# Rotary pair swap of q and k: a VectorE lane shuffle in place of a TensorE permutation matmul, with q and k of layers 3 and 4 laid out so that the two members of a pair lie 16 lanes apart

## What is computed

```python
def apply_rope(x, cos, sin):                       # layers 1 and 2
    n_freq = HEAD_DIM // 4                         # 16
    xf = x.astype(jnp.float32).reshape(*x.shape[:-1], 2, 2, n_freq)
    x1, x2 = xf[..., 0, :], xf[..., 1, :]          # pairs lie 16 apart
    cb, sb = cos[None, :, None], sin[None, :, None]
    out = jnp.stack([x1 * cb - x2 * sb, x2 * cb + x1 * sb], axis=-2)
...
def apply_rope_2(t, cos, sin):                     # layers 3 and 4
    half = QK_DIM // 2                             # 32
    t1, t2 = t[..., :half], t[..., half:]          # pairs lie 32 apart
    return jnp.concatenate([t1 * cos - t2 * sin, t2 * cos + t1 * sin], axis=-1)
```

## Time and profile before

| | |
|---|---|
| three runs | 2384.16, 2387.83, 2380.02 us; median 2384.16 |
| profiled execution | span 2381.0 us (the page gives no other time for it) |
| TensorE busy | 2312.4 us, 97% of the span |
| VectorE busy | 1349.6 us, 57% |
| ScalarE busy | 1077.6 us, 45% |
| DMA | 335.97 MB, 141 GB/s in the mean |
| mean granted TensorE clock | 0.992 |

### The profile page before, as it was taken

How to read it: one execution, slowest core, us unless ns; L and a number is a source line. 1 busy time by engine, 2 the same in 40 slices (tenths; PEclk the granted TensorE clock), 3 DMA queues, 4 the chain that set the end, 5 groups by cost and what they waited for, 6 DMA issues and landing times.

```text
span 2381.0 us, 36140 instructions
## 1 busy us (share of the span) xinstructions
PE 2312.4 (97%) x14230; PEld 1894.7 (80%) x14230; DVE 1349.6 (57%) x2393; ACT 1077.6 (45%) x2066; POOL 33.5 (1%) x40
## 2 busy tenths in 40 slices
PE   8999999999889999999999999999999999999999
PEld 6658878778857999777667788888888887798888
DVE  5454432333646767577886434534434778756776
ACT  4343422223545555545556423522323765655543
POOL 0300000000100000000000000000000000000000
PEclk9999999999999999999999999999999999999999
DMA  8473333333365555255554322222222222154554
GB/s 312 169 272 110 98 115 124 115 126 105 107 230 178 195 177 179 92 197 191 196 207 151 106 97 84 85 98 98 97 95 92 89 89 72 58 164 151 188 184 151
DMA packets 95319, 335.97 MB, mean 141 GB/s; under 512 B 10672, under 2 KB 12720, under 8 KB 95024
## 3 DMA queue, kind: packets, MB, share of 16 engines
q1 hardware_dynamic: 95152, 333.67, 41.3%
HBM read 332.58 MB, written 1.05 MB: 140 GB/s over the span
## 4 chain that ended last, share of the span: by engine, by line
PE 85%; DVE 6%; ACT 5%; issue 2%; DMA 2%; SPq 0%; ACTq 0%; DVEq 0%
PE out L1443 19%; PE out L1444 19%; PE out L1445 19%; PE out L1437 7%; PE out L1441 3%; PE sc L1516 2%; DVE w_lo L1852 2%; DMA raw<-stream 2%; PE pt L1525 1%; PE out L1381 1%; PE pv L1543 1%; ACT w_hi L1582 1%; PE pv L1541 1%; PE pt L1381 1%; PE aux L1341 1%
## 5 line engine op out<-in xcount | busy, mean ns | idle before, releaser
L1443 PE MATMUL out<-act,w_lo 128*128 128x512 f32 (+1 forms) x1816 | 650.3, 358 | 8.8 <-DVE w_lo L1852 3.1
L1582 ACT CAST w_hi<-raw 128x1024 fp32r<-128x1024 f32 (+2 forms) x444 | 453.0, 1023 | 411.5 <-PE out L1445 337.5
L1444 PE MATMUL out<-act,w_hi 128*128 128x512 f32 (+1 forms) x1816 | 637.5, 351 | 0.0
L1445 PE MATMUL out<-act,w_hi 128*128 128x512 f32 (+1 forms) x1816 | 637.1, 351 | 0.0
L1852 DVE TENSOR_TENSOR w_lo<-raw,w_hi 128x1024 fp32r<-128x1024 f32 (+2 forms) x444 | 528.4, 1193 | 126.6 <-ACT w_hi L1582 126.4
L1443 PEld LDWEIGHTS out<-act,w_lo 128*128 128x128 f32 x1816 | 345.5, 190 | 65.3 <-issue 13.3
L1445 PEld LDWEIGHTS out<-act,w_hi 128*128 128x128 f32 x1816 | 345.3, 190 | 45.5
L1444 PEld LDWEIGHTS out<-act,w_hi 128*128 128x128 f32 x1816 | 345.7, 190 | 43.5
L1443 PE MATMUL out<-mix,w_lo 128*128 128x512 f32 (+1 forms) x734 | 261.2, 356 | 1.0 <-DVE mix L2157 1.0
L1444 PE MATMUL out<-mix,w_hi 128*128 128x512 f32 (+1 forms) x734 | 260.1, 354 | 0.0
L1445 PE MATMUL out<-mix,w_hi 128*128 128x512 f32 (+1 forms) x734 | 260.0, 354 | 0.0
(11 more groups left out here) (281 smaller groups left out, 2883.2 us busy)
## 6 DMA issues: line engine op xcount, KB each, us to landing
raw<-stream SPq DMA_DIRECT2D x604, 512.0 KB, 3.5
raw<-stream SPq DMA_DIRECT2D x16, 384.0 KB, 3.1
raw<-stream SPq DMA_DIRECT2D x16, 256.0 KB, 2.7
x<-xin SPq DMA_DIRECT2D x4, 512.0 KB, 5.7
consts<-const SPq DMA_DIRECT2D x1, 1344.0 KB, 8.2
x<-ctx SPq DMA_DIRECT2D x1, 1024.0 KB, 5.9
out<-x SPq DMA_DIRECT2D x8, 128.0 KB, 1.7
consts<-const SPq DMA_DIRECT2D x1, 320.0 KB, 5.6
```

The source lines that it names most:

```text
L1443: nc.tensor.matmul(ps, wl, xh, start=(k == 0), stop=False)
L1444: nc.tensor.matmul(ps, wh, xl, start=False, stop=False)
L1445: ins = nc.tensor.matmul(ps, wh, xh, start=False, stop=(k == s.nk - 1))
L1582: nc.scalar.copy(w_hi[:, number % HL, 0:n], raw[:, place[number] % RAW, 0:n]).then_inc(S["hi_ready"], 1)
```

## The change

Each of the 42 permutation matmuls goes. VectorE first multiplies `qg` by a table of signed sines into `turn`, then moves the lanes: a stream shuffle with the pattern `lane ^ 16` inside each group of 32 lanes writes `turned`, which is added to the cosine product. That needs the two members of a pair in one group of 32 lanes. In layers 0 and 1 they are; in layers 2 and 3 the columns of `w_q` and `w_k` and the two gains are put in another order (`HALVES_IN`) by the host, which also lets all layers share one pair of tables. The constants shrink from 640 to 384 columns in the first load and from 2688 to 2176 in the second. The banks `pt` and `pv` have no slot for the swap any more, and the steps no wait for one.

```diff
     def query_sum(q):
-        s = step("qsum", q=q, n=q.n, ready=q.rel, block=q.layer // 2)
+        s = step("qsum", q=q, n=q.n, ready=q.rel)
         use_aux(s)
         last[q.sq, 0] = ("aux_ready", s.aux_value)
         s.guess = signal("q_guess")
+        s.product = signal("sin_ready")
         s.turned = signal("turn_ready")
-        turn_place(s, q)
...
+        opposite = [lane ^ 16 for lane in range(32)]
...
-                    sp.dma_start(consts[:, 0:5 * P], const[:, 0:5 * P]).then_inc(S["const_in"], 16)
+                    sp.dma_start(consts[:, 0:3 * P], const[:, 0:3 * P]).then_inc(S["const_in"], 16)
...
                 elif s.kind == "rstd" and not s.nested:
                     sum_squares(s)
-                    if s.q:
-                        wait(pe, s.pt_free)
-                        nc.tensor.matmul(turn_banks[s.pt], swap[s.block], qg[:, s.q.qg, 0:NX], start=True, stop=True)\
-                            .then_inc(S["turn_ready"], 1)
...
-                    wait(pe, s.pt_free)
-                    nc.tensor.matmul(turn_banks[s.pt], swap[s.block], qg[:, s.q.qg, 0:NX], start=True, stop=True)\
-                        .then_inc(S["turn_ready"], 1)
...
-                        dve.wait_ge(S["turn_ready"], s.turned[1])
-                        nc.vector.tensor_tensor(turn[:, :], rope_s[s.block], turn_banks[s.pt], ALU.mult).then_inc(S["turn_read"], 1)
+                        dve.wait_ge(S["out_act"], s.q.rel[1])
+                        nc.vector.tensor_tensor(turn[:, :], qg[:, s.q.qg, 0:NX], rope_s, ALU.mult).then_inc(S["sin_ready"], 1)
                 elif s.kind == "qsum":
                     g = qg[:, s.q.qg, 0:NX]
                     dve.wait_ge(S["out_act"], s.q.rel[1])
+                    nc.vector.tensor_tensor(turn[:, :], g, rope_s, ALU.mult).then_inc(S["sin_ready"], 1)
                     wait(dve, s.q.dst_free)
-                    nc.vector.tensor_tensor(q_t[:, s.q.slot, 0:NX], g, rope_c[s.block], ALU.mult)
-                    dve.wait_ge(S["turn_ready"], s.turned[1])
-                    nc.vector.tensor_tensor(turn[:, :], rope_s[s.block], turn_banks[s.pt], ALU.mult).then_inc(S["turn_read"], 1)
+                    nc.vector.tensor_tensor(q_t[:, s.q.slot, 0:NX], g, rope_c, ALU.mult)
+                    dve.wait_ge(S["sin_ready"], s.product[1])
+                    nc.vector.stream_shuffle(turned[:, :], turn[:, :], opposite).then_inc(S["turn_ready"], 1)
                 elif s.kind == "qrope":
                     dst = q_t[:, s.q.slot, 0:NX]
-                    dve.wait_ge(S["turn_read"], s.r.turned[1])
-                    nc.vector.tensor_tensor(dst, dst, turn[:, :], ALU.add).then_inc(S["qk_ready"], 1)
+                    dve.wait_ge(S["turn_ready"], s.r.turned[1])
+                    nc.vector.tensor_tensor(dst, dst, turned[:, :], ALU.add).then_inc(S["qk_ready"], 1)
...
                 elif s.kind == "turn":
                     g = qg[:, s.q.qg, :]
-                    link(nc.vector.tensor_tensor(g[:, 0:NX], g[:, 0:NX], rope_c[s.block], ALU.mult))
-                    link(nc.vector.tensor_tensor(g[:, 0:NX], g[:, 0:NX], turn[:, :], ALU.add))
+                    dve.wait_ge(S["sin_ready"], s.r.product[1])
+                    nc.vector.stream_shuffle(turned[:, :], turn[:, :], opposite).then_inc(S["turn_ready"], 1)
+                    link(nc.vector.tensor_tensor(g[:, 0:NX], g[:, 0:NX], rope_c, ALU.mult))
+                    dve.wait_ge(S["turn_ready"], s.turned[1])
+                    link(nc.vector.tensor_tensor(g[:, 0:NX], g[:, 0:NX], turned[:, :], ALU.add))
...
+            if mat in ("w_q", "w_k"):
+                a = a[:, np.concatenate([HALVES_IN, HD + HALVES_IN])]
...
+HALVES_IN = np.arange(HD).reshape(2, 2, 16).transpose(1, 0, 2).reshape(-1)
```

More of the change, by code:

```diff
@@ L189, in qk_block @@
         return s
-    def turn_place(s, q):
-        if q.layer == 2:
-            s.pt, s.pt_free = "pv", last.get(("pv", 0))
-            last["pv", 0] = signal("turn_read")
-        else:
-            s.pt, s.pt_free = take("pt", 2, signal("turn_read"))
     def query_sum(q):
-        s = step("qsum", q=q, n=q.n, ready=q.rel, block=q.layer // 2)
+        s = step("qsum", q=q, n=q.n, ready=q.rel)
         use_aux(s)
@@ L230, in rstd @@
         if q:
-            s.block = q.layer // 2
-            s.turned = signal("turn_ready")
-            turn_place(s, q)
+            s.product = signal("sin_ready")
         return s
@@ L253, in qk_turn @@
     def qk_turn(r, between=lambda: None):
-        step("turn", q=r.q, block=r.q.layer // 2)
+        s = step("turn", q=r.q, r=r)
+        s.turned = signal("turn_ready")
         between()
@@ L261, in qk_finish @@
         spread_rows(r, done)
-        s = step("rope", q=q, n=q.n, dst=dst, slot=slot, dst_free=dst_free, norm_done=r.spread, block=q.layer // 2)
+        s = step("rope", q=q, n=q.n, dst=dst, slot=slot, dst_free=dst_free, norm_done=r.spread)
         s.done = last["qg", q.qg] = done
@@ L1185, in build @@
         turn = sb("turn", [P, NX])
+        turned = sb("turned", [P, NX])
         smax = sb("smax", [P, 2, 4])
@@ L1205, in build @@
         ident, ones, heads = part(P), part(P), part(P)
-        swap = [part(P), part(P)]
-        rope_c, rope_s = [part(NX), None], [part(NX), None]
-        rope_c[1], rope_s[1] = part(NX), part(NX)
+        rope_c, rope_s = part(NX), part(NX)
         dft = part(2 * 2 * NX).rearrange("p (j n) -> p j n", j=2)
@@ L1238, in build @@
         banks = {"aux": aux, "sc1": scb[1]}
-        turn_banks = {0: ptb[0][:, 0:NX], 1: ptb[1][:, 0:NX], "pv": pvb[:, NX:NT]}
+        opposite = [lane ^ 16 for lane in range(32)]
         def col(layer, name, j=0, n=1):
@@ L1248, in build @@
             o_mean o_guess ox_ready ox_hi ln_sum ln_sq ln_x ln_h s_done ln_done vec_in cond_in lam_in const_in ctx2_in small_in stored part_mods
-            silu_ready turn_ready turn_read dve_seq act_seq pool_seq bank_zero lam_ready sum_exp q_guess q_norm conv_ready""".split()
+            silu_ready sin_ready turn_ready dve_seq act_seq pool_seq bank_zero lam_ready sum_exp q_guess q_norm conv_ready""".split()
         S = {n: ctx.enter_context(nc.semaphore(n)) for n in names}
@@ L1287, in _ @@
                 if r == 17 + AHEAD:
-                    sp.dma_start(consts[:, 5 * P:], const[:, 5 * P:]).then_inc(S["const_in"], 16)
+                    sp.dma_start(consts[:, 3 * P:], const[:, 3 * P:]).then_inc(S["const_in"], 16)
                     sp.dma_start(small[:, :, :], wsmall).then_inc(S["small_in"], 16)
@@ L1459, in _ @@
                     for _ in range(s.n):
-                        nc.tensor.matmul(pvb[:, 0:NX], ones, consts[:, 5 * P:5 * P + NX], start=True, stop=True)
+                        nc.tensor.matmul(pvb[:, 0:NX], ones, consts[:, 3 * P:3 * P + NX], start=True, stop=True)
                 elif s.kind == "qsum":
@@ L2306, in constants @@
     d = p % HD
-    tables = []
-    for reach, axis in ((16, d // 32), (32, (d % 32) // 16)):
-        second = (d // reach) % 2 == 1
-        swap = np.zeros((P, P), f)
-        swap[p[second] - reach, p[second]] = 1
-        swap[p[~second] + reach, p[~second]] = -1
-        parts.append(swap)
-        angle = pos[axis] * inv_freq[d % 16][:, None]
-        tables += [np.cos(angle), np.sin(angle)]
-    parts += tables
+    angle = pos[d // 32] * inv_freq[d % 16][:, None]
+    second = (d // 16) % 2 == 1
+    parts += [np.cos(angle), np.where(second[:, None], -np.sin(angle), np.sin(angle))]
     turn = 2 * np.pi * np.outer(t, t) / NX
@@ L2353, in pack_vectors @@
             put(layer, "g2", tiles(inputs["norm2_g_2"][i]))
-            put(layer, "qg", np.tile(inputs["q_norm_g_2"][i], 2)[:, None])
-            put(layer, "kg", np.tile(inputs["k_norm_g_2"][i], 2)[:, None])
+            put(layer, "qg", np.tile(inputs["q_norm_g_2"][i][HALVES_IN], 2)[:, None])
+            put(layer, "kg", np.tile(inputs["k_norm_g_2"][i][HALVES_IN], 2)[:, None])
             put(layer, "b_gate", tiles(inputs["b_gate_2"][i]))
```

## The result

The changed kernel takes 2371.14 us (median of 4 runs, 2369.00 to 2372.42) against 2385.78 us for the kernel before (4 runs, 2380.02 to 2387.83): a ratio of 0.9940, 95% interval 0.9924 to 0.9957, some 14 us less. The forecast was 2371. The profiled execution took 2372.1 us, with a span of 2370.3 us, 10.7 us less than the profiled one of before.

A forecast was written before the change was run, and what follows sets the result against it. The prediction took TensorE, busy 97% of the span, as the bound. Gains of 3.6 + 0.3 + 3.8 + 4.5 + 0.5 = 12.7 us, the last for constants, took 2384.2 to 2371.5, predicted as 2371, range 2359 to 2382.

The forecast's parts named there:

- The slot: TensorE's queue: each of 42 swaps takes 0.51 us, taken as 0.5; 21 us leave, the most this term gives.
- the prediction's other estimate: TensorE's swap priced from four fp32 passes at 256 columns and 2.4 GHz: 0.43 us each, 17.9 us for 42.
- The shuffle: VectorE: one new 128 x 256 shuffle per tile at 0.45 us, bounds 0.32 and 1.22.
- rival (b): VectorE: shuffle dear or loading its pattern each time, about 15 exposed, nearly all given back; gain under 7 us; chance 0.22.
- Layer 0: Five tiles, -3.6 us: 2.5 from slots, 1.1 more because the first scores' wait for rotated q goes.
- Layer 1: Five tiles, -0.3 us: four slots lost in waits, one gives 0.5, two shuffles on the chain to the scores cost 0.2.
- One sign in the forecast: Head of layer 1: its first scores would not come earlier, unlike layer 0's, which come about 1.6 us earlier.
- Layer 2: Sixteen tiles, -3.8 us: keys keep 4.0, first two queries 1.0, six others lose 1.2 to waits for streamed blocks.
- Rival (d): TensorE's clock: lengthened waits bring half-clock stretches costing 1.3 us each, 19 us over 15 places, so 2390; chance 0.03.
- Layer 3: Sixteen tiles, -4.5 us: five pairs held by `n_r` give 0.5 each, two others 1.0, the head 0.
- About 0.3 net: Layer 3, VectorE from the maxima to `n_r`: the key's shuffle costs about 0.3 us net of overlap, leaving `n_r` 0.5 earlier.
- (a): All layers: the named TensorE waits don't grow and all is kept; 24 us gained, so 2360; chance 0.15.

The follow-up runs named there:

- the kernel before with both moves: Kernel before, swap matmuls kept, with taps at each group's start and, in layer 2, none between a query's swap and its sum: 2374.92 us, ratio 0.9970.
- the last experiment: Changed kernel with taps at group starts, none between layer 2's query shuffle and sum, and one instead of three between key shuffle and norm: 2358.49 us.
- the taps first: Changed kernel with VectorE's convolution taps at the start of each group instead of its end: 2372.07 us, ratio 0.9950 to the kernel before.
- both moves: Changed kernel with taps at each group's start and, in layer 2, none between a query's shuffle and its sum: 2365.30 us, ratio 0.9921.

## Why the prediction was right, point by point

That the total was right within a us is in part luck. The sum said 12.7 us; the profiles show 10.7 and 11.2, the medians 14.6, and the kernel before itself moved by 1.6 us when a fourth run was added. By stretch, the start came out 2.9 us short and layer 2 1.4 to 1.8 short, layer 3 gave 1.1 more, and 1.4 us came where nothing had been changed.

**The slot: right for the queries of layer 3, mis-sized elsewhere.** The step `0.32 + (0.42 - 0.23) = 0.51` compared with the steady distance of 0.227 us. But the first w_lo behind the key's sums takes 0.32 us by itself. Kernel before and changed kernel, layer 3:

```profile
1952.57 0.50 PE L1465 MATMUL aux<-consts,sq 128*128 128x2 f32 x4
...
1953.54 1.13 PE L1516 MATMUL sc<-k_t,q_t 64*128 64x512 f32 x4
...
1955.10 0.95 PE L1327 MATMUL aux<-consts 128*128 128x2 f32 x8
...
1956.66 0.39 PE L1444 MATMUL out<-act,w_hi 128*128 128x512 f32 x1
```

```profile
1948.73 1.02 PE L1317 MATMUL aux<-consts 128*128 128x2 f32 x8
1949.61 0.48 PE L1433 MATMUL out<-act,w_lo 128*128 128x512 f32 x1
1949.93 0.40 PE L1434 MATMUL out<-act,w_hi 128*128 128x512 f32 x1
```

With the row at 1947.11 above: at the query, sums to scores took 0.97 us and take 1947.11 - 1946.68 = 0.43: the slot is 0.54. At the key, scores to the first w_hi took 1956.66 - 1953.54 = 3.12 us and take 1949.93 - 1947.11 = 2.82: 0.30. Between the two kernels whose TensorE is busy all the time here, the kernel before with both moves and the one of the last experiment, the steps differ by 0.53 to 0.55 at all seven queries and by 0.26 or 0.27 at five of the seven keys (0.08 and 0.32 at the others); that is the cleanest price. In layer 2, from the sums to the first `w_hi` behind them, queries and keys alike took 1.56 us and take 1.13: 0.43, the prediction's other estimate, and 0.51 only at the one key that is followed by transposes. With the idle matmuls put back the 1.56 us are back too. So what a slot costs depends on the matmul behind it. At the key of layer 3 the transposes and sums take 0.13 us longer once the swap is gone (0.06 to the start of the sums, 0.07 in them); with the idle matmul they take the old time. Why is open. By these prices (16 tiles of layer 2 at 0.43, 8 queries at 0.54 and 8 keys at 0.30 in layer 3, the ten others at some 0.5) the slots sum to an estimate of 19 us, not 21.

**The shuffle: right.** 0.44 us against 0.45. The Trainium skill (VectorE: DVE Perf Modes, the perf-mode tier table) gives it the same 1x mode as an fp32 `tensor_tensor`, by which the estimate was the 0.42 us of a product; the trace is 0.02 above that. The pattern loads of rival (b) do come, at 12 to 14 ns. The Trainium skill (Vector Engine (DVE) Microarchitecture Reference, The reshape front-end and per-opcode configuration) says that the pattern stays until the next load; that 41 of these loads are needless would follow, but no run here leaves them out.

**Layer 0: right in kind.** The timeline of VectorE and the first scores:

```profile
69.27 0.96 DVE L2010 TENSOR_TENSOR turn<-qg,consts 128x256 f32<-128x256 f32 x1
70.15 1.31 DVE L2012 TENSOR_TENSOR q_t<-qg,consts 128x256 f32<-128x256 f32 x1
...
71.39 0.44 DVE L2014 STREAM_SHUFFLE turned<-turn 128x256 f32<-128x256 f32 x1
71.86 0.82 DVE L2019 TENSOR_TENSOR q_t<-q_t,turned 128x256 f32<-128x256 f32 x1
```

```profile
73.22 1.13 PE L1499 MATMUL sc<-k_t,q_t 64*128 64x512 f32 x4
```

The wait of 1.09 us is gone, as predicted, and the products double beside GpSimd. But the scores are only 0.03 us earlier, because this execution was 2 us behind at 48 us. The seven profiles whose layer 0 is that of the changed kernel have their first scores 0.03, 0.08, 0.33, 0.55, 1.03, 1.31 and 2.11 us ahead of 73.25; the three with that of before 0, -0.24 and -3.49. The means are 0.8 and -1.2: 2.0 us between them, where 1.6 + 0.5 was predicted. At 175 us it is 3.2 instead of 4.1. With such a spread ten profiles agree with the term; they don't show it.

**Layer 1: 0.3 predicted, 0.4 and 0.6 measured, by another way.** One sign in the forecast failed: the first scores of layer 1 did come earlier, by a further 1.0 us against those at 175 us, mostly because TensorE's wait for q fell from 1.19 to 0.53 us. VectorE's chain without the wait for the swap (1.04 us) is shorter by more than the shuffle and the doubled product add. Behind it the wait for the block at 664 us took most of it back: 3.05 us before, 3.32 and 4.26 in the two profiles of after, with 6.8 us of half clock from 661 us on where it had been 3.4 from 666 on.

**Layer 2: the mis-sized term, 3.8 against 2.0 and 2.4.** `8 x 0.5` for the keys was 3.0: 0.52 at the first, nothing at the second, whose slot went into a wait for a block, and 0.39 to 0.43 at the six others. Of the first two queries, booked at 1.0, one kept 0.42; with the other, at 1014 us, the step lost 0.95, which is the next point. For the queries from 1106 us on the mechanism was right, that TensorE runs into a streamed block, and its size was not: "TensorE leaves this point 0.2 us later" counted part of the shuffle, which is hidden behind `w_hi`. What happens is simpler: the block lands at nearly the same distance behind the sums as before, so the slot of 0.43 becomes waiting (0.45 to 0.97 us at the tile of the earlier trace rows), and the step neither gains nor loses much: -0.39, -0.11, -0.01, -0.10 and -0.04 in the five. The sixth, at 1060 us, kept 0.17. That is -0.5 us for the six, where -1.2 was booked.

**The clock.** Behind the wait of 2.76 us at 1010 us TensorE ran at half clock for 6.8 us in both profiles of after, against 3.4 in the earlier trace rows. Changed kernel, and the last one, where that wait is 1.19 us:

```profile
1009.30:1012.70 3.40, 2.97 (x13) 2.95 (x14) 3.37 (x7) 0.86 (x2) 0.00 (x0) 0.50 0.93 342
1012.70:1016.10 3.40, 3.40 (x9) 2.64 (x8) 3.37 (x10) 3.03 (x9) 0.00 (x0) 0.50 0.49 194
```

```profile
1005.00:1012.00 7.00, 7.00 (x35) 5.88 (x35) 6.90 (x15) 4.42 (x12) 0.00 (x0) 1.00 0.68 268
```

The step there lost 0.95 us; in the kernel without the shuffles, with 3.4 us of half clock, it gained 0.49, about a slot. So 3.4 us more of half clock cost 1.4 us. Rival (d) had a price of 1.3 us, close to that, and the wrong place: in layers 2 and 3 the waits that the change lengthened brought no half clock, one that was there already did, for longer. The kernels with the slots put back and without the shuffles had 3.4 us there, the second profile of before and the one with two shuffles 6.8, so the length isn't the change's alone. Nor does a shorter wait decide it: the two kernels of the taps first and of both moves waited 1.44 us there without a half clock, and the kernel before with both moves waited the same 1.44 us and had one of 3.4 us. And a wait for a block of 2.11 us, without taps in the query part, had 6.8 us of half clock behind it at 1117.6, which is what (d) feared.

The clock also made the 0.5 us between 1303 and 1873 us, where no tile was changed. Kernel before, then changed kernel:

```profile
1512.30:1515.70 3.40, 3.40 (x9) 2.65 (x9) 3.40 (x6) 3.20 (x5) 0.00 (x0) 0.50 0.55 172
```

```profile
1845.60:1849.00 3.40, 3.40 (x18) 3.40 (x18) 1.70 (x5) 2.01 (x8) 0.00 (x0) 0.50 0.33 128
```

The first of these has no counterpart in the changed kernel, which gained 1.6 us there; the second, 6.8 us long, has none in the kernel before, and 1.1 us was lost.

**Layer 3: 5.6 against 4.5.** The chain was followed rightly to the maxima: VectorE is held by `q_sq`, and they start 3.98 us behind the sums where it was 4.89: 0.91 earlier, 0.76 predicted. "About 0.3 net" for the key's shuffle was 0.08. So `n_r` keeps pace with TensorE, the wait stays at 0.24 us instead of growing to 0.8, the other at 0.81, and every slot is kept at its own price: seven times 0.54 + 0.27 is 5.7, and 5.6 was measured. The forecast had also read the pairs as tighter than they were. It held five of the seven to be bound by `n_r`; in the kernel before `n_r` was only just ready (0.05 us ahead of its reader) at two, and 0.23 to 0.25 us early at three more. In the changed kernel it is only just ready at five, and TensorE still waits for it at one alone. The head, booked at 0, gave 0: the wait for `q_ms` grew from 0.74 to 1.17 us, and one of 0.43 us for `n_r` appeared. The two rows of 140 us above say the same: TensorE is busy for 136.93 us of them before and after, so the waits took the same share of a shorter layer.

**The rivals.** (a) assumed that the waits don't grow: true in layer 3, false in layer 2. Of (b), the formula 12.7 - 15 x (S - 0.45) fits at 0.88 us (it says 6.5 us less gain, and 6.1 to 7.0 was measured) and fails at 0: it says 6.8 us more gain than at 0.45, and none could be told.

## What to carry to other kernels

Removing work from the busiest engine gives its slot only where what it then waits for comes earlier too: follow both chains to the same point and compare the engine that binds each (`w_hi` on ScalarE here, not the VectorE instruction in view). Price a slot by what stands between the same two neighbours with and without it, not against a steady row. And where two edits of an order compete for one queue, try them together before dropping either: here 0 and -6 us made +6, and a third 5 to 7 more. When two traces are compared, set the stretches in which nothing was changed beside the others: here they differed by 1.4 us, with other stretches of half clock in them.

## What the runs showed of the hardware

The kernel before spread over 11 us in 45 runs, 2378.6 to 2389.7, and the mean granted clock goes with it: 18 runs at 0.991 have a mean of 2385.2 us, 12 at 0.993 one of 2381.9. Two profiles of one program can thus differ by 5.2 us with layer 3 the same to 0.02 us, so a difference between two profiles has to be read stretch by stretch, with the clock beside it.

A product of two SBUF operands took up to 0.96 us and once 1.31 beside GpSimd's branch, against 0.42 alone. The Trainium skill (SBUF — State Buffer, on the shared port pair) speaks of exclusion for the whole instruction; the trace agrees in direction, and in size it shows a doubling to a tripling.
